# A fused decoder step: expert biases, the sample rows of the gather and the layout of the down weights in the expert loop

## The reference

```python
logits = h @ w_router + b_router
top_v, top_e = lax.top_k(logits, 4)
gate = softmax(top_v)
gu  = xb @ w_gu[e] + b_gu[e]
gt  = minimum(gu[:, :1024], 7.0)
up  = clip(gu[:, 1024:], -7.0, 7.0)
act = (up + 1.0) * gt * sigmoid(1.702 * gt)
y   = act @ w_dn[e] + b_dn[e]
x   = x + g2 * sum over a token's 4 experts of gate * y
```

## Time and profile before

| | us |
|---|---|
| median of 3 runs | 1877.17 |
| lowest and highest | 1874.58, 1880.96 |
| span of the profiled execution | 1876.8 |
| start of the first item (gather of item 0) | 791.2 |
| end of the last item's down bias | 1853.5 |
| PE busy | 1735.9 |
| DVE busy, ACT busy | 513.5, 361.0 |

### The profile page before, as it was taken

How to read it: one execution, slowest core, us unless ns; L and a number is a source line. 1 busy time by engine, 2 the same in 40 slices (tenths; PEclk the granted TensorE clock), 3 DMA queues, 4 the chain that set the end, 5 groups by cost and what they waited for, 6 DMA issues and landing times.

```text
span 1876.8 us, 24465 instructions
## 1 busy us (share of the span) xinstructions
PE 1735.9 (92%) x9532; PEld 919.0 (49%) x9532; DVE 513.5 (27%) x1062; ACT 361.0 (19%) x722; POOL 24.4 (1%) x18
## 2 busy tenths in 40 slices
PE   6998587899979999699999999999999999999996
PEld 4777587467646778433333333333333333333332
DVE  1554766631120102412111121211212121121213
ACT  2222121112231110221112112111111211111122
POOL 0000300000000000000000000000000000000000
PEclk8997899999999999799999999999999999999998
DMA  9537302143417996179999999999999999999990
GB/s 405 222 126 321 135 10 127 73 171 123 152 48 269 352 345 264 45 299 392 366 398 374 384 383 379 394 371 388 376 387 388 372 396 364 394 375 386 397 359 24
DMA packets 83882, 541.19 MB, mean 288 GB/s; under 512 B 7122, under 2 KB 11346, under 8 KB 61170
## 3 DMA queue, kind: packets, MB, share of 16 engines
q1 hardware_dynamic: 83106, 534.65, 72.2%
q0 software_dynamic: 720, 5.76, 0.8%
HBM read 533.54 MB, written 6.84 MB: 288 GB/s over the span
## 4 chain that ended last, share of the span: by engine, by line
PE 83%; DVE 8%; ACT 3%; DMA 2%; SPq 2%; issue 1%; POOL 0%; DVEq 0%; ACTq 0%
PE banks L487 24%; PE banks L524 12%; PE banks L1101 6%; PE banks L451 5%; PE banks L753 5%; PE banks L473 4%; PE banks L502 3%; PE banks L460 2%; DMA ring<-wpre 2%; PE banks L529 2%; PE banks L949 2%; PE banks L497 2%; PE banks L974 2%; DVE regC L1671 1%; DVE regB L581 1%
## 5 line engine op out<-in xcount | busy, mean ns | idle before, releaser
L487 PE MATMUL banks<-ring,regA 128*64 128x512 f32 x2048 | 455.0, 597 | 0.8 <-ACT regA L540 0.8
L487 PEld LDWEIGHTS banks<-ring,regA 128*64 128x64 f32 x2048 | 141.6, 137 | 282.2 <-issue 281.5
L524 PE MATMUL banks<-ring,regC 128*64 128x512 f32 x1024 | 226.8, 595 | 0.0
L581 DVE TENSOR_TENSOR regB<-regB,banks 128x528 f32<-128x528 f32 x132 | 87.2, 701 | 433.6 <-PE banks L473 433.6
L524 PEld LDWEIGHTS banks<-ring,regC 128*64 128x64 f32 x1024 | 70.7, 137 | 131.8 <-issue 127.9
L600 DVE TENSOR_SCALAR regA<-banks 128x512 f32<-128x512 f32 x32 | 22.1, 691 | 375.8 <-PE banks L502 375.8
L451 PE MATMUL banks<-regC,regA 128*64 128x512 f32 (+1 forms) x396 | 98.7, 616 | 3.8 <-DVE regA L573 3.8
L473 PE MATMUL banks<-regA,regC 64*128 64x264 f32 x528 | 82.8, 424 | 12.6 <-DVE regB L581 11.9
L753 PE MATMUL banks<-hT,ring 128*128 128x264 f32 x384 | 90.3, 391 | 0.0
L545 ACT ACTIVATE regA<-regA 128x512 f32<-128x512 f32 x32 | 20.1, 629 | 337.2 <-DVE regA L600 337.2
L753 PEld LDWEIGHTS banks<-hT,ring 128*128 128x128 f32 x384 | 71.5, 190 | 18.2 <-issue 6.8
(11 more groups left out here) (432 smaller groups left out, 1888.5 us busy)
## 6 DMA issues: line engine op xcount, KB each, us to landing
ring<-w_gu SPq DMA_DIRECT2D x128, 2048.0 KB, 11.1
ring<-w_dn SPq DMA_DIRECT2D x64, 2048.0 KB, 9.7
ring<-wpre SPq DMA_DIRECT2D x41, 2048.0 KB, 13.2
ring<-kvT SPq DMA_DIRECT2D x64, 256.0 KB, 4.8
ring<-kv SPq DMA_DIRECT2D x64, 256.0 KB, 6.1
ring<-ssm SPq DMA_DIRECT2D x2, 2048.0 KB, 10.9
o_ssms<-ring POOLq DMA_DIRECT2D x2, 2048.0 KB, 9.3
con_sb<-con SPq DMA_DIRECT2D x1, 1269.0 KB
```

Source lines behind the costliest of these rows:

```text
L487: mm = pe_mm(bank[x // 2][SLOT * (x % 2):SLOT * (x % 2 + 1), :], lhsT=hg[:, k % 4, SLOT * (k // 4):SLOT * (k // 4 + 1)], rhs=ring[c][:, 20 ...
L524: mm = pe_mm(bank[5][SLOT * y:SLOT * (y + 1), :], lhsT=actT[:, m % 4, SLOT * (m // 4):SLOT * (m // 4 + 1)], rhs=ring[c][:, D * (m % 4) + H ...
L581: V.tensor_tensor(pair, pair, banks[:, b:b + 2, 0:T], ALU.add).then_inc(acc_added, 1)
```

## The change

In the loads, a partition of a down chunk now takes four consecutive rows of w_dn, 16 KB in one piece. To match, the turns of the activations take every fourth column (`act_[:, q::4]`). The bias load becomes two loads an item, the gate bias to partition 0 and the up bias to partition 32, 2 KB pieces, without the down bias.

The down biases of all experts are loaded once into `ytok` (expert e on partitions e and 64 + e), and `selT` starts as the gate matrix (expert by token, on the same partitions), so the scatter that runs in item 0 adds every token's gated down biases. L529 is gone.

The gate/up biases become four matmuls of 1 row by 64 columns, on array rows 0 to 31 for the gate and 32 to 63 for the up half. The sample rows of the gather lie on partitions 64 to 71 and are gathered first, right behind the biases, on array rows 64 to 95. The waits for `acc_added` and `sel_new` stand ahead of the biases.

The turn of `selg` moves from behind the scatter to behind the gather, into bank 6, and covers all 128 partitions for the sample tile (zeros elsewhere). `turn_gathered` moves ahead of all four turns of the activations. On ScalarE the copy of `selT` moves behind the copy of `gtok`, and the copy of `hg` ahead of both copies of `actT`. On VectorE `selg` now waits for the copy of the previous `selT`.

Ahead of the loop: three more matmuls bring the gates to partitions 64 and up, two more copies fill `selT`, the zeroing of `selT`, `ytok` and the sample tile of `selg` moves from the start of the loop to earlier places, and the transposes of the sample rows become plain matmuls.

```diff
-        brow = cut(regC, 8100, 3 * 512)
+        brow = cut(regC, 8100, 2 * 512)
...
-        wdn = t["w_dn"].rearrange("e (m p) n -> e p m n", p=P)
-        tok_tiles = ((0, P), (1, P), (2, NSA))
+        wdn = t["w_dn"].rearrange("e (c p r) n -> e c p (r n)", c=2, p=P)
+        SROW = slice(64, 64 + NSA)
+        tok_tiles = ((0, slice(0, P)), (1, slice(0, P)), (2, SROW))
...
-                    src = wdn[bass.ds(e, 1), :, 4 * (c - 4):4 * (c - 3), :].rearrange("a p m n -> p (a m) n")
-                    sp.dma_start(ring[c][:, :].rearrange("p (m n) -> p m n", m=4), src).then_inc(slot_in[c], 16)
+                    src = wdn[bass.ds(e, 1), c - 4, :, :].rearrange("a p n -> p (a n)")
+                    sp.dma_start(ring[c][:, :], src).then_inc(slot_in[c], 16)
...
-                sp.dma_start(brow[0:2, :], t["biases"][bass.ds(e, 1), :, :].rearrange("a h n -> h (a n)")).then_inc(brow_in, 16)
+                for u in range(2):
+                    sp.dma_start(brow[32 * u:32 * u + 1, :].rearrange("a (h n) -> a h n", h=2),
+                                 t["biases"][bass.ds(e, 1), :, HALF * u:HALF * (u + 1)]).then_inc(brow_in, 16)
...
+            sp.wait_ge(ytok_copied, 1)
+            for y in range(2):
+                sp.dma_start(ytok[SLOT * y:SLOT * y + NE, :],
+                             t["biases"][:, y:y + 1, 2 * HALF:3 * HALF].rearrange("e a n -> e (a n)")).then_inc(stage("rest_in"), 16)
...
+            def gather_tile(i, r, first):
+                for y in range(2):
+                    mm = pe_mm(bank[2][SLOT * y:SLOT * (y + 1), :], lhsT=self_[r, i, :],
+                               rhs=h2tok[r, i, 4 * y:4 * y + 4, :].rearrange("p k c -> p (k c)"),
+                               start=first, stop=(i == 1), skip_group_check=True)
+                return mm
+            def gather_prompt():
+                for i in range(2):
+                    mm = gather_tile(i, slice(0, P), False)
                 mm.then_inc(gathered, 1)
...
                     if c == 0:
                         scatter(j)
-                        pe.wait_ge(selg_new, j + 1)
-                        for i, r in tok_tiles:
-                            mm = pe_mm(bank[4][:, P * i:P * i + r], lhsT=selg[0:r, i, :, :].rearrange("p a s -> p (a s)"),
-                                       rhs=ident[0:r, 0:r], start=True, stop=True)
-                        mm.then_inc(selT_turned, 1)
-                pe.wait_ge(brow_in, j * 16 + 16)
-                for x in range(2):
-                    pe_mm(bank[x][:, :], lhsT=both, rhs=brow[0:2, HALF * x:HALF * (x + 1)], start=False, stop=True,
-                          skip_group_check=True).then_inc(gu_ready, 1)
+                pe.wait_ge(brow_in, j * 32 + 32)
                 pe.wait_ge(acc_added, j * 4 + 5)
-                gather(j + 2)
-                pe.wait_ge(selT_copied, j + 2)
+                pe.wait_ge(sel_new, j + 2)
+                for x in range(4):
+                    u, y = x // 2, x % 2
+                    mm = pe_mm(bank[u][SLOT * y:SLOT * (y + 1), :], lhsT=ones[32 * u:32 * u + 1, 0:SLOT],
+                               rhs=brow[32 * u:32 * u + 1, HALF * y:HALF * (y + 1)], start=False, stop=True, skip_group_check=True)
+                    if y == 1:
+                        mm.then_inc(gu_ready, 1)
+                gather_tile(2, SROW, True)
+                gather_prompt()
+                pe.wait_ge(selg_new, j + 1)
+                for i in range(2):
+                    pe_mm(bank[6][:, P * i:P * (i + 1)], lhsT=selg[:, i, :, :].rearrange("p a s -> p (a s)"),
+                          rhs=ident, start=True, stop=True)
+                pe_mm(bank[6][:, NPR:T], lhsT=selg[:, 2, :, :].rearrange("p a s -> p (a s)"),
+                      rhs=ident[:, SROW], start=True, stop=True).then_inc(selT_turned, 1)
+                turn_gathered(j + 2)
                 pe.wait_ge(act_ready, j + 1)
                 for y in range(2):
                     for q in (2 * y, 2 * y + 1):
-                        mm = pe_mm(bank[4 - 2 * y][:, P * q:P * (q + 1)], lhsT=act_[:, P * q:P * (q + 1)], rhs=ident, start=True, stop=True)
+                        mm = pe_mm(bank[4 - 2 * y][:, P * q:P * (q + 1)], lhsT=act_[:, q::4], rhs=ident, start=True, stop=True)
                     mm.then_inc(a_turned, 1)
-                    if y == 0:
-                        turn_gathered(j + 2)
...
-                pe_mm(bank[5][:, :], lhsT=both, rhs=brow[0:2, 2 * HALF:3 * HALF], start=False, stop=True, skip_group_check=True).then_inc(moe_read, 1)
...
+                dve.wait_ge(selT_copied, j + 1)
                 for i, r in tok_tiles:
-                    ins = V.tensor_scalar(selg[0:r, i, :, :], iota[0:r, :].unsqueeze(1).to_broadcast([r, 2, SLOT]),
+                    ins = V.tensor_scalar(selg[r, i, :, :], iota[r, :].unsqueeze(1).to_broadcast([r.stop - r.start, 2, SLOT]),
...
+            V.memset(ytok[:, :], 0.0).then_inc(ytok_copied, 1)
...
+            link(V.memset(selT[:, :], 0.0))
+            link(V.memset(selg[:, 2, :, :], 0.0))
...
+                mm = pe_mm(bank[0][SLOT:SLOT + NE, a:b], lhsT=gate[0:b - a, i, :], rhs=ident[0:b - a, 0:b - a], start=True, stop=True,
+                           skip_group_check=True)
...
+            link(V.tensor_copy(selT[0:NE, :], bank[0][0:NE, 0:T]))
+            V.tensor_copy(selT[SLOT:SLOT + NE, :], bank[0][SLOT:SLOT + NE, 0:T]).then_inc(selT_copied, 1)
```

More of the change, by code:

```diff
@@ L444, in moe_tensor @@
             K = number_of_items(pe)
-            def gather(n):
-                pe.wait_ge(sel_new, n)
-                for i, r in tok_tiles:
-                    for y in range(2):
-                        mm = pe_mm(bank[2][SLOT * y:SLOT * (y + 1), :], lhsT=self_[0:r, i, :],
-                                   rhs=h2tok[0:r, i, 4 * y:4 * y + 4, :].rearrange("p k c -> p (k c)"),
-                                   start=(i == 0), stop=(i == 2), skip_group_check=True)
+            def gather_tile(i, r, first):
[7 more added lines that the diff above has]
+                    mm = gather_tile(i, slice(0, P), False)
                 mm.then_inc(gathered, 1)
@@ L476, in moe_tensor @@
             pe.wait_ge(stage("rg_copied"), 1)
-            gather(1)
+            pe.wait_ge(sel_new, 1)
+            gather_tile(2, SROW, True)
+            gather_prompt()
             turn_gathered(1)
+            pe.wait_ge(stage("rest_in"), 80)
             def item(j):
@@ L541, in item @@
             def item(j):
-                act.wait_ge(selT_turned, j + 1)
-                A(selT[:, :], bank[4][:, 0:T], ACT.Copy).then_inc(selT_copied, 1)
                 act.wait_ge(gmin_ready, j + 1)
@@ L547, in item @@
                 A(gtok[:, :], bank[2][:, :], ACT.Copy).then_inc(gtok_copied, 1)
+                act.wait_ge(selT_turned, j + 1)
+                A(selT[:, :], bank[6][:, 0:T], ACT.Copy).then_inc(selT_copied, 1)
+                act.wait_ge(g_turned, j + 2)
+                A(hg[:, :, :], bank[3][:, :].rearrange("p (q s) -> p q s", q=4), ACT.Copy).then_inc(hg_ready, 1)
                 for y in range(2):
@@ L1198, in _ @@
                     for k in range(4):
-                        mm = pe.transpose(bank[q % 4][0:b - a, k * P:(k + 1) * P], hT[:, 4 * y + k, a:b], ident)
+                        if i < 2:
+                            mm = pe.transpose(bank[q % 4][:, k * P:(k + 1) * P], hT[:, 4 * y + k, a:b], ident)
+                        else:
+                            mm = pe_mm(bank[q % 4][SROW, k * P:(k + 1) * P], lhsT=hT[:, 4 * y + k, a:b], rhs=ident, start=True, stop=True)
                     mm.then_inc(stage("h2_turned"), 1)
```

35 lines of the change are left out of this document (15 added, 20 removed).

## The result

| | us |
|---|---|
| before, median of 4 runs | 1879.07 (1874.58 to 1881.38) |
| changed, median of 4 runs | 1800.57 (1797.33 to 1805.18) |
| ratio, 95% interval | 0.9581 (0.9559 to 0.9603) |
| profiled execution of the changed kernel, span | 1801.05, 1799.2 |
| forecast, range | 1774, 1765 to 1812 |

A forecast was written before the change was run, and what follows sets the result against it. TensorE was taken to bound the expert loop; 1.15 + 0.86 + 0.97 + 0.3 = 3.3 us an item, times 32 = 105 us, so 1876.8 - 105 + 0.8 + 1 = 1774 us, range 1765 to 1812.

The forecast's parts named there:

- rival B: Activation turns on TensorE: reading every fourth float slows their weight loads; 1793 us if by half, 1811 if doubled; chance 0.08.
- What bounds the kernel: Expert loop: TensorE sets the item of 32.93 us, with 31.6 us of DMA work close behind.
- Down bias: TensorE, end of the item: L529 goes with its change of array shape, 1.15 us an item less.
- Gate/up biases: TensorE, L502: four quarter-sized matmuls side by side take 1.05 us instead of 1.91, 0.86 us an item less.
- sample tile: TensorE's gather: the sample tile runs beside the biases on its own row group, 0.97 us an item less.
- Rival A: Biases and gather: part of the tiles do not run side by side; 1801 or 1829 us; chance 0.13.
- The turns: TensorE, gather's end to down projection: reordered turns take 2.93 us, gain 0.3 us an item.
- Ahead of the loop: Routing before the expert loop: added copies, matmuls and zeroing, less zeroings that go, cost 0.8 us more in all.
- the 1 us added for the queue: Loop's DMA queue: allowance for transfers lagging TensorE, with some 20 us in hand at the first items; 1 us in all.
- The transfers: Loop's DMA: w_dn in 16 KB pieces runs at 425 GB/s, so 29.6 us an item instead of 31.6, tying with TensorE.
- Rival C: Loop's DMA: w_dn stays slow and the transfers bound the loop at 31.6 us an item; 1823 us; chance 0.12.
- VectorE's new wait, the bank, the table load, SP's extra load: Expert loop: the selT wait, bank 6, one ScalarE table load less and a second bias load, all costed at nothing.

The follow-up runs named there:

- perm_write: Changed kernel, but VectorE's last step writes the activations in the order of the turns, so TensorE loads contiguous columns; 1772.35 us, run again 1774.33.
- route_light: perm_write with the three added gate matmuls behind the three transposes and the two added selT copies later; 1777.75 us, run again 1769.14.
- before_rows16k: Kernel before with only the new 16 KB layout of the down weights and its strided turns; 1901.57 us, ratio 1.0136.
- rows4k: Changed kernel with the old 4 KB layout of the down weights and contiguous turns; 1783.36 us, ratio 0.9497.
- before_no_down_bias: Kernel before with the down bias left out of the result and L529 gone, nothing in its place; 1846.87 us, ratio 0.9828.

## Why the prediction was right and where it was wrong

- By its own signs: an item of 30.30 us and 3.72 us from the gather's end to L539 are not the 29.5 to 29.8 and 2.9 that it named as right, and 1.86 us for L528 is over the 1.3 that it named as the sign of rival B. The start of L511 and L454 together, L498 behind L539 without a gap and the DMA share of 0.99 are as it said. That the time fell into the range is owed to the room that was left for rival B, not to the forecast's case.
- What bounds the kernel: right. TensorE set the item before and sets it after.
- Down bias, 1.15 us an item: 1.20 with this part alone.
- Gate/up biases (0.86) and the sample tile (0.97) side by side: right, 1.02 us for all six tiles where 1.05 was taken, and the gather at 1.88 where 2.90 - 0.97 = 1.93 was. Undoing each costs 0.83 and 0.99. Rival A falls.
- The turns: this is the step that failed. "TensorE itself needs 0.67 + 1.16 + 1.16 for its own eight turns" priced the four activation turns like those of `gtok`. They take 1.86. The stretch from the gather's end to L539 is 3.72 us, not 2.93, and the item 30.30, not 29.65. Rival B was the case, with 0.08 of the chance: 1.86 - 1.09 = 0.77 us more for four turns, between its two prices (1793 if the loads slowed by half, 1811 if they doubled; by 71% they did, which is 1774 + 25 = 1799). The mistake was in the weighing: "the two kinds of turn otherwise have one shape" took the shape for the whole of the price, while the step in memory is the one thing that set them apart. Without the step the item is 29.47 us (perm_write), 0.18 below the 29.65 of the sum; over 32 items that is 6 us, which hides the next point there. That perm_write's 1772.35 is so near 1774 is in part these two errors cancelling.
- Ahead of the loop 0.8 us was counted. In the traces the way from the token counts to the first gate/up matmul went from 20.5 to 25.1 us, 4.6 more. 0.7 of it is up to the gate transposes; 1.6 lies in the stretch with the three added matmuls, which alternate with transposes (route_light, which also moves the copies, got 1.2 of all this back); 0.4 is VectorE's part up to the first gather; 1.9 comes after the gather has begun. The first gather, chain line of before and then of the changed kernel, there with one of the added matmul pairs ahead:

```profile
791.23 4.58 PE banks L451 x12
```

```profile
782.00 0.56 PE banks L1233 x2
...
794.57 5.61 PE banks L454 x12
```

  It takes 1.0 us more, and the turns behind it the rest: the granted clock stood at 0.50 (1.2 GHz) from 790 to 800 us where before it was 0.67 there on the mean, partly back at 2.4 GHz. "Its first gather costs the same tiles" was true of the tiles and not of the clock. Behind it, the first 8 gate/up matmuls of the loop took 6.35 us where before they took 5.09, 1.3 us more.
- Together: 0.654 x 32 = 20.9 for the item (the turns cost 0.83 more than counted, the rest 0.18 less), 3.8 for the routing, 1.3 for the first gate/up matmuls, 0.7 because the routing began later in this execution, less 0.4 behind the loop and the 1 us added for the queue: 25.3 of the 25.2 us between 1774 and the span of 1799.2.
- The transfers: the conclusion was right (no DMA wait), and so was the pace of 29.6 us an item in pieces of 16 KB (29.69 in perm_write). The price that it put on the old layout was wrong. "In pieces of 4 KB, 334 at 0.93" was read as the price of the pieces. The windows of before, 3 us each, show where the slow stretch lies:

```profile
857.00:860.00 3.00, 3.00 (x19) 1.43 (x19) 0.00 (x0) 0.87 (x2) 0.00 (x0) 1.00 1.02 437
860.00:863.00 3.00, 3.00 (x17) 1.00 (x14) 0.00 (x0) 0.00 (x0) 0.00 (x0) 1.00 0.55 197
863.00:866.00 3.00, 3.00 (x13) 0.78 (x10) 0.00 (x0) 0.19 (x1) 0.00 (x0) 1.00 0.96 339
866.00:869.00 3.00, 3.00 (x16) 0.86 (x12) 0.00 (x0) 1.69 (x2) 0.00 (x0) 1.00 1.03 385
```

  The engines run dry at 860 to 863, since all six buffers are full until the first down chunk is read, and the load that then starts moves at 339 GB/s before it picks up. The changed kernel shows such a dip with 16 KB pieces: 333 GB/s at 863 to 866, 425 on the way to the next such place. In before_rows16k, with 16 KB pieces alone, the share times the item is again 31.6 us. And in rows4k, where the engines do not run dry, 4 KB pieces go at 422 overall. That the dips come of the empty queue is read from where they lie and are missing; why a load is slow there, no run shows. What the layout is worth is 30.11 - 29.69 = 0.42 us of transfer an item. It made 11 us from rows4k to perm_write, and only because rows4k runs into the transfers and perm_write just does not; in the change itself it was a loss of 17 us, since it brought the strided turns. The rule of 512 B from the Trainium skill, DMA: Bandwidth & Descriptors, Specifications, is nearer to this than the forecast was, though 0.42 us an item are left for the pieces. Rival C would have needed 31.6 us an item to be fixed; before_no_down_bias at 31.72 without a wait leaves that open, and rows4k, held by its transfers at 30.11, shows that it is not.
- VectorE's new wait, the bank, the table load, SP's extra load: cost nothing, as said. VectorE had 10.75 us idle ahead of its first step.

## What to carry to other kernels

Price an instruction by its shape and by its step in memory: when a new layout of data in one place is paid for with a strided read in another, look for that read on the engine that sets the time, and move the rearrangement to an engine with slack, as perm_write does. Small matmuls that share an array shape and lie on different row groups and column halves cost here what one of them costs (1.02 us for six), and conversely leaving out one half of such a pair gained nothing. When an item is already close to the pace of its transfers, compare how long ahead of its use each load lands, item by item: a head start that shrinks by 0.22 us an item hides for a whole loop that the transfers are the slower part. A transfer rate that is read from a stretch in which the queue has just run dry is no rate for a stretch in which it never does.

## What the runs showed of the hardware that was not expected

- A weight load of 128 by 128 in fp32 with a step of 16 bytes took 329 ns against 192; the stretch of 8 such records in the chain took 1.86 us against 1.09 for the turns of `gtok`. VectorE's product over 512 columns took 1118 ns with the same step on both reads, and 1061 with a step of 128 floats in the write, against 693 in the kernel before.
- Six tiles of the array, three row groups by two column halves, ran at once at the price of one: 1.02 us for the six, 1.05 for L529 alone.
- The DMA work of an item is not a constant: the same loads in the same pieces came to 0.96 x 32.92 = 31.6 us in the kernel before, where the queue ran dry once an item, and needed 30.1 us in rows4k, where it did not. In pieces of 16 KB it was 0.94 x 33.58 = 31.6 us in before_rows16k and 29.7 in perm_write.
- The start of the routing moved by up to 10.6 us between the profiled executions of kernels that are alike ahead of it, more than the 1.2 us by which one of them was improved.
